# Gate products of a second expert stage: one fp32 product, or two rounded ones

## The reference, cut to what matters

```python
def peer(h, w_q, sub_keys, u, v):
    ...
    i1 = jnp.take_along_axis(si[:, :, 0], fi // PEER_TOPK, axis=-1)
    i2 = jnp.take_along_axis(si[:, :, 1], fi % PEER_TOPK, axis=-1)
    idx = (i1 * PEER_NKEYS + i2).reshape(T, PEER_HEADS * PEER_TOPK)
    g = jax.nn.softmax(fv, axis=-1).reshape(T, PEER_HEADS * PEER_TOPK).astype(h.dtype)
    ...
        act = jax.nn.gelu(jnp.einsum('td,ted->te', hc, ue), approximate=False)
        return jnp.einsum('te,ted->td', gc * act, ve)
```

## Time and profile before

| | us |
|---|---|
| median of 3 runs | 4283.16 (4282.72 to 4296.16) |
| span of the profiled execution | 4284.8 |
| PE busy | 4186.1 (98%), 24253 instructions |
| DVE busy | 3070.5 (72%) |
| ACT busy | 1794.5 (42%) |
| POOL busy | 1331.5 (31%) |
| all gate products (L1574), both stages | 157.3 us of PE |

### The profile page before, as it was taken

One profiled execution on the slowest core, in us unless ns is written; L12 is line 12 of the kernel. 1 busy time (PEld: TensorE's weight loads), 2 busy tenths in 40 slices (PEclk: granted clock), 3 DMA queues, 4 the chain that ended last, 5 costly groups with the idle time before them and its releaser, 6 DMA issues.

```text
span 4284.8 us, 61360 instructions
## 1 busy us (share of the span) xinstructions
PE 4186.1 (98%) x24253; PEld 3726.7 (87%) x24253; DVE 3070.5 (72%) x4932; ACT 1794.5 (42%) x2979; POOL 1331.5 (31%) x699
## 2 busy tenths in 40 slices
PE   8999999999999999999999999999999999999999
PEld 5888778888888799867999999999999799998887
DVE  5775557877887676465589798788887675554676
ACT  3233352233233544264244776333334645444444
POOL 0000200000000100000378666777772058444443
PEclk9999999999999999999999999999999999999999
DMA  6543215544555365212477899999994156778885
GB/s 273 224 166 144 87 40 206 220 180 188 220 200 199 113 247 191 79 40 70 145 242 254 291 345 348 367 363 353 357 355 164 60 199 220 226 245 285 282 286 181
DMA packets 286591, 926.87 MB, mean 216 GB/s; under 512 B 19680, under 2 KB 170336, under 8 KB 212192
## 3 DMA queue, kind: packets, MB, share of 16 engines
q1 hardware_dynamic: 249440, 788.70, 51.7%
q0 software_dynamic: 36864, 134.23, 8.7%
HBM read 837.92 MB, written 84.93 MB: 215 GB/s over the span
## 4 chain that ended last, share of the span: by engine, by line
PE 87%; DVE 5%; DMA 3%; ACT 2%; POOL 1%; issue 1%; SPq 0%; ACTq 0%; POOLq 0%; DVEq 0%
PE bank L1136 25%; PE bank L1137 25%; PE bank L1138 25%; PE bank L1574 3%; PE bank L1329 1%; PE bank L1131 1%; PE bank L1126 1%; PE bank L1122 1%; PE bank L1341 1%; POOL weight_ring_low L2964 1%; PE bank L1366 1%; DMA gates<-work 1%; DVE work L2701 1%; DVE weight_ring_low L2282 1%; ACT work L1884 0%
## 5 line engine op out<-in xcount | busy, mean ns | idle before, releaser
L2964 POOL TENSOR_TENSOR weight_ring_low<-weight_ring,up_high 128x1024 fp32r<-128x1024 f32 x233 | 587.6, 2527 | 1065.0 <-ACT up_high L2030 1063.4
L1138 PE MATMUL bank<-peer_h_high,weight_ring_low 128*128 128x256 f32 (+2 forms) x2240 | 699.0, 312 | 0.0
L1136 PE MATMUL bank<-peer_h_high,up_high 128*128 128x384 f32 (+1 forms) x2048 | 643.7, 314 | 13.7 <-POOL weight_ring_low L2964 9.2
L1137 PE MATMUL bank<-h_low,up_high 128*128 128x384 f32 (+1 forms) x2048 | 634.5, 310 | 0.0
L2117 ACT ACTIVATE down_high<-weight_ring 128x1024 fp32r<-128x1024 f32 x256 | 257.0, 1052 | 525.9 <-PE bank L1138 525.9
L1138 PE MATMUL bank<-h_high,weight_ring_low 128*128 128x512 f32 (+1 forms) x1280 | 464.2, 363 | 0.0
L1136 PE MATMUL bank<-h_high,in_high 128*128 128x512 f32 (+1 forms) x1216 | 441.4, 363 | 0.3
L1137 PE MATMUL bank<-h_low,in_high 128*128 128x512 f32 (+1 forms) x1216 | 441.0, 363 | 0.0
L2928 POOL TENSOR_SCALAR h<-work,params 128x256 f32<-128x256 f32 x12 | 11.8, 997 | 1377.9 <-PE bank L1481 874.8
L1138 PEld LDWEIGHTS bank<-peer_h_high,weight_ring_low 128*128 128x128 f32 x2240 | 426.8, 191 | 3.8
L2728 DVE TENSOR_TENSOR weight_ring_low<-weight_ring,down_high 128x1024 fp32r<-128x1024 f32 x128 | 310.6, 2427 | 161.8 <-ACT down_high L2117 161.8
(11 more groups left out here) (424 smaller groups left out, 10081.1 us busy)
## 6 DMA issues: line engine op xcount, KB each, us to landing
weight_ring<-in_up SPq DMA_DIRECT2D x128, 1024.0 KB, 5.5
weight_ring<-in_down SPq DMA_DIRECT2D x128, 1024.0 KB, 6.3
weight_ring<-in_mod_w SPq DMA_DIRECT2D x112, 1024.0 KB, 5.0
weight_ring<-in_ffn_in SPq DMA_DIRECT2D x88, 1024.0 KB, 6.9
weight_ring<-in_ffn_out SPq DMA_DIRECT2D x64, 704.0 KB, 5.3
gates<-work SPq DMA_DIRECT2D x40, 1024.0 KB, 9.8
gelu<-work SPq DMA_DIRECT2D x64, 384.0 KB, 6.8
work<-gates SPq DMA_DIRECT2D x32, 768.0 KB, 12.6
```

Of the source, the lines that this page charges most:

```text
L1136: mm(dst, w_high, a_high, start=first, stop=False)
L1137: mm(dst, w_high, a_low, start=False, stop=False)
L1138: return mm(dst, w_low, a_high, start=False, stop=last)
L2964: G.tensor_tensor(ring_low[:, slot, w], ring[:, slot, w], up_high[:, n % 3, :].bitcast(F32), ALU.subtract)\
```

## The change

In the second stage, the gate product of a token becomes two rounded products that add up in the same place of the bank: the one-hot of the second key (`exact_second`, exact in fp32r) by the first key's one-hot times the gate's rounded high part (`exact_first`), and by the one-hot times the gate's low part (`low_mark`). `split_gates` makes the two parts of all gates once, at the start. The new tiles lie in the places of the old marks and of memory that is free there; no semaphore is new. The first stage stays as it is.

```diff
+        exact_first = high_low("exact_first", [P, 2, SUB, P], work_at)
+        exact_second = high_low("exact_second", [P, 2, SUB, P], work_at, 2 * SUB * P)
+        low_mark = high_low("low_mark", [P, 2, SUB, P], work_at, down_at)
+        gate_high = high_low("gate_high", [P, TL], work_at, down_at + HP * NKEYS + TL)
+        gate_low = work[:, down_at + HP * NKEYS:down_at + HP * NKEYS + TL]
...
-                            i = mm(ps[bank][:, k * P:k * P + P], second_mark[:, q % 2, 4 * c + k], first_mark[:, q % 2, 4 * c + k],
-                                   start=True, stop=True)
+                            dst, token = ps[bank][:, k * P:k * P + P], 4 * c + k
+                            if l == 1:
+                                mm(dst, exact_second[:, q % 2, token], exact_first[:, q % 2, token], start=True, stop=False)
+                                i = mm(dst, exact_second[:, q % 2, token], low_mark[:, q % 2, token], start=False, stop=True)
+                            else:
+                                i = mm(dst, second_mark[:, q % 2, token], first_mark[:, q % 2, token], start=True, stop=True)
...
-                    V.tensor_tensor(second_mark[:, q % 2], every, spread(routed[:, 1, tokens], 2, P), ALU.is_equal)
+                    second = exact_second if l == 1 else second_mark
+                    V.tensor_tensor(second[:, q % 2], every, spread(routed[:, 1, tokens], 2, P), ALU.is_equal)
...
-                    V.tensor_tensor(first, first, spread(routed[:, 2, tokens], 2, P), ALU.mult).then_inc(marks_weighted, 1)
+                    V.tensor_tensor(low_mark[:, q % 2], first, spread(gate_low[:, tokens], 2, P), ALU.mult)
+                    V.tensor_tensor(exact_first[:, q % 2], first, spread(gate_high[:, tokens].bitcast(F32), 2, P), ALU.mult)\
+                        .then_inc(marks_weighted, 1)
+
+                def split_gates():
+
+                    steps.wait()
+                    link(V.tensor_copy(gate_high[:, :], routed[:, 2, 0:TL]))
+                    link(subtract(gate_low, routed[:, 2, 0:TL], gate_high[:, :]))
...
+                if l == 1:
+                    split_gates()
                 marks(0)
```

More of the change, by code:

```diff
@@ L691, in build @@
         gate_tiles = {1: take(2, NKEYS, BLOCK)}
+        exact_first = high_low("exact_first", [P, 2, SUB, P], work_at)
[3 more added lines that the diff above has]
+        gate_low = work[:, down_at + HP * NKEYS:down_at + HP * NKEYS + TL]
+        assert 2 * SUB * P == HP * NKEYS and HP * TOPK == TL
         at8 = lambda n: work[:, HP * T:HP * T + n]
```

## The result

The changed kernel takes 4298.62 us (median of 22 runs, 4291.97 to 4307.29), the kernel before in the same sessions 4294.51 us (22 runs): a ratio of 1.0014, with a 95% interval of 1.0008 to 1.002, or 6.0 us more (3.4 to 8.6). The median forecast was 4288 us and the range ended at 4298: the time lies 0.6 us above it.

The account below looks back on a forecast made before the run. TensorE, busy 98% of the span, was taken as the bound. Records 0, steady DVE work 0, start +5 us: 4284.8 + 5 = 4289.8 us span, median forecast 4288 us; 4280 to 4298 us holds eight in ten.

Parts of the forecast that it names:

- The records: Gate product on PE, second stage: 512 rounded records replace 512 fp32 ones at the same 0.111 us weight-load pitch; 0 us.
- The Trainium skill's rule on the passes: Gate product: true fp32 is four passes, so two rounded passes take half the time; 28 us less, not adopted.
- The second multiply, steady part: DVE, each half block: one more 1.15 us multiply fits in 6.6 us idle per block; 0 us.
- The start: Start of the gate part: rounding, subtraction and two multiplies delay the first DVE weight split; +5 us, from 3.0 to 7.2.
- the two holds that made the upper bound: Start of the gate part: CAST and one more multiply each held 2.1 us by POOL; 7.2 us in all.
- the 1.3 to 5 us of the text: First gates: forecast length of PE's wait for the marks of the first half block.
- The wait for the DVE split: Start of the gate part: PE was to wait longer than 1.45 us for the first weight unit DVE splits.
- the bound of 0.3%: Whole kernel: 12.8 us, about what a measurement can tell from no change; three runs lay within 13.4 us.
- the column line (1): Rival on the gate records: columns decide, pitch 0.067 us, PE saves 23 us, less 5 at the start, 4265 us; chance 0.10.
- the fp32 rate for short records (2): Rival on the gate records: each short rounded product takes 0.223 us, PE loses 57 us, 4345 us; chance 0.07.
- The outcome that was given 0.81: Whole kernel: time stays the same, within 0.3%; faster had 0.09, slower 0.10.
- Rival 3: Gate part: held multiplies and POOL splits make PE wait every half block; 4320 us with 2 us a block; chance 0.03.

Follow-up runs that it names:

- e9_clean_start: Changed kernel with the first two half blocks in fp32 and POOL splitting the first two blocks' weight unit in DVE's place; 4294.01 us, 1.0002 to the kernel before.
- e8_best: Changed kernel with bf16 one-hots and gate parts, first two half blocks in fp32, POOL splitting DVE's weight unit in the first two blocks; 4275.5 us, ratio 0.9955.
- e7_warm: Changed kernel, with PE doing 40 rounded products of 256 columns where it waits for the first half block's marks; 4300.07 us, 1.0013 to the kernel before.
- e1_late_start: Changed kernel with the first two half blocks in fp32 with a single multiply, and gates split only after the first DVE weight split; 4295.69 us, ratio 1.0007.
- e6_half_columns: As e1_late_start, but products from the third half block on move only the first 64 columns of the marks; 4292.32 us, one run.

## Why the prediction was right or wrong

- *The records* (0 us): right, and for the reason given. Two records for two, group for group: the half blocks went from 7.54 to 7.55 us. The pitch at 128 columns is the weight load's: unchanged with half the moving columns, 0.059 us with half the weights, 0.056 us with bf16. The Trainium skill's rule on the passes (FP8 and Floating Point Precision, TensorE Precision Notes), by which 28 us would have gone as an estimate, does not give the time here, as the passes were not what the time was spent on.
- *The second multiply, steady part* (0 us): right for this kernel (e9_clean_start, 0.02 us). The margin was thin: with POOL's added splits PE waited 1.2 us (e9_clean_start), and with half blocks 0.8 us shorter as well, 5.2 us (e8_best).
- *The start* (+5 us, from 3.0 to 7.2): the delay on DVE was right, and closely so: its first split came 5.05 us later behind the routing. The reason was right in part. Of the two holds that made the upper bound, the CAST's came (2.23 us for 0.28); the other did not come on top, since one multiply was held before and one after the change, only not the same. The marks were 5.37 us late, over the 1.3 to 5 us of the text, which its own terms would have put at 5.5 (1.3 and two holds of 2.1). The wait for the DVE split, forecast to be longer than 1.45 us, was 0.87 us with the clock kept up (e7_warm) and gone without: PE reached it later, as it had waited for the marks.
- *The term put at nothing*: the forecast priced the wait at its own length and gave no price to the clock behind it. Behind the idle 5.4 us PE ran at half clock for some 9 us: from the first group to the second it took 3.8 us more than the 7.79 us of before without its wait. Of these, 2.8 us are on top of what the start costs with the clock up (8.1 us in the gate part, 5.3 in e7_warm); the rest covers the wait for the split.
- *The sum and the range*: +5 us forecast, +6.0 measured (3.4 to 8.6). The step that failed by most is the last one of the sum, "so the median forecast is 4288 us": it hung the difference on the median of three runs, 4283.16 us, while the same kernel's 22 runs have 4294.51 us. With that base and the +5 us it would have been 4299.5 us; with the old base and the clock's 2.8 us it would have been 4291, still inside the range. A range of 10 us above the forecast had no room for the base's own scatter, 13 us in three runs, which the text had read out but used only for the bound of 0.3%. That the difference by the runs (+6.0) is so near to +5 is in part luck: the profiles have +8.1 us in the gate part and +7.1 in the span.
- *The rivals*: the column line (1) and the fp32 rate for short records (2) are both out by the pitch of 0.108 to 0.111 us. The outcome that was given 0.81, within 0.3%, is the one that came. Rival 3 did not show in this kernel: PE waits for no marks after the first.

Open is why the clock fell behind the 3.27 us of waiting ahead of the down product before, and not after: profiles of either kind are among the kernels here, and none of the experiments was made for it. Open too is why the first three runs of the kernel before were so low. Part of its scatter goes with the clock: in the 23 runs beside e7_warm, seven with a mean granted clock of 0.993 took 4290.9 us on average, four with 0.991 took 4299.1 us; for the first three no such list is on record. And only the profiles show the clock's 2.8 us.

## What to carry to other kernels

Before a product is cut into fewer passes, look at what its records are spaced by: if a record with one moving column has the same spacing, it is the weight load, and what helped here was fewer, narrower or 2-byte weights. Price a new wait of a busy TensorE at more than its length, because it may run at the lower clock behind it (here 3.8 us behind a wait of 5.37). Take the base of a forecast from as many runs as its range needs. And look for all that stands between a late arrival and the first instruction that needs it. When a step gets shorter, the engine that kept up with it has less room: here the wait moved from the first block to the second and the third, each time to a split that stood behind DVE operations held by POOL, until one operand was put in another memory.

## What the runs showed of the hardware that was not expected

- Rounded 32-bit weights of 128 columns: 0.108 to 0.111 us from record to record, with 128 or with 64 moving columns; 64 columns of weights: 0.059 us; bf16 weights and moving side, 128 columns of each: 0.056 us. The load's row shows 192, 134 and 98 ns.
- Behind 5.37 us of waiting the granted clock was 0.50 for the next 8 us, with PE busy 7.71 of them; with 40 spare products in the wait it stayed 1.00. Behind a wait of 1.91 us it was 0.50 in one kernel's profile (e1_late_start) and 1.00 in another's (e6_half_columns).
- While POOL had an operation under way, a DVE multiply or subtraction with both inputs in the work memory took up to 3.4 us instead of 1.2, and a CAST from work memory to work memory 2.2 instead of 0.3; a multiply with one input in a bank took 1.22 in all 30 cases.
